# Naming the first layer's experts by a matrix product, and making the top-six mask by one comparison, in a two-layer diffusion transformer block

## The reference, cut to what matters

```python
def moe_ffn(h, router_w, router_bias, w_gu, w_down, shared_gu, shared_down):
    scores = jax.nn.sigmoid(jnp.dot(h, router_w, preferred_element_type=jnp.float32))
    _, idx = lax.top_k(scores + router_bias.astype(jnp.float32), TOP_K)       # TOP_K = 6 of 64
    gates = jnp.take_along_axis(scores, idx, axis=-1)
    gates = gates / jnp.sum(gates, axis=-1, keepdims=True) * ROUTED_SCALE
    ...
    def expert_block(args):
        src_b, gate_b, e = args
        y = swiglu(h_pad[src_b], w_gu[e], w_down[e])                          # 1024 -> 2*384 -> 1024
        return y * gate_b[:, None].astype(y.dtype)
    ...
    return routed + swiglu(h, shared_gu, shared_down)
```

## Time and profile before

| what | us |
|---|---|
| median of 3 runs (lowest, highest) | 2533.88 (2532.23, 2536.08) |
| the profiled execution | 2537.54 |
| its span in the trace | 2535.7 |
| TensorE matmul busy, whole span | 2305.1 |
| VectorE busy, whole span | 792.5 |
| mean DMA rate over the span | 301 GB/s |

### The profile page before, as it was taken

One profiled execution on the slowest core, in us unless ns is written; L12 is line 12 of the kernel. 1 busy time (PEld: TensorE's weight loads), 2 busy tenths in 40 slices (PEclk: granted clock), 3 DMA queues, 4 the chain that ended last, 5 costly groups with the idle time before them and its releaser, 6 DMA issues. The chain is left out here.

```text
span 2535.7 us, 40724 instructions
## 1 busy us (share of the span) xinstructions
PE 2305.1 (91%) x17170; PEld 1241.6 (49%) x17170; DVE 792.5 (31%) x1709; ACT 403.7 (16%) x860; POOL 229.0 (9%) x286
## 2 busy tenths in 40 slices
PE   6999899999877888888897998899999999999998
PEld 2456744454333343334343556755655565555553
DVE  2375745262110101111112546753222222212123
ACT  2323344110000000000001233352000000000000
POOL 0007200011101111110001005300000000000000
PEclk9999999999999999999998999999999999999999
DMA  8000197359999999999997310015999999999997
GB/s 333 34 17 36 65 379 305 135 226 413 427 426 417 417 419 417 417 419 399 385 422 303 129 50 21 28 47 212 404 390 377 376 423 367 429 412 424 408 416 297
DMA packets 86042, 762.18 MB, mean 301 GB/s; under 512 B 14376, under 2 KB 14904, under 8 KB 27232
## 3 DMA queue, kind: packets, MB, share of 16 engines
q1 hardware_dynamic: 74720, 734.30, 70.3%
q0 software_dynamic: 11136, 25.20, 2.6%
HBM read 748.54 MB, written 23.49 MB: 304 GB/s over the span
## 5 line engine op out<-in xcount | busy, mean ns | idle before, releaser
L1675 PE MATMUL banks<-arena,htreg 128*32 128x384 f32 (+2 forms) x5312 | 749.0, 521 | 119.0 <-DMA arena<-in_exp_w_gu 113.8
L1675 PEld LDWEIGHTS banks<-arena,htreg 128*32 128x32 f32 (+2 forms) x5312 | 331.7, 132 | 527.4 <-issue 435.1
L1700 PE MATMUL banks<-arena,modreg 128*32 128x512 f32 (+2 forms) x1992 | 351.6, 597 | 20.4 <-issue 19.1
L2556 DVE TENSOR_TENSOR modreg<-modreg,banks 128x384 f32<-128x384 f32 x65 | 36.0, 554 | 687.1 <-ACT modreg L2056 687.1
L1700 PEld LDWEIGHTS banks<-arena,modreg 128*32 128x32 f32 (+2 forms) x1992 | 117.4, 126 | 222.1 <-issue 220.7
L1715 PEld LDWEIGHTS banks<-htreg,hreg 128*128 128x128 f32 x800 | 194.2, 334 | 8.7 <-issue 5.9
L1715 PE MATMUL banks<-htreg,hreg 128*128 128x128 f32 x800 | 191.5, 398 | 0.0
L1196 PE MATMUL banks<-arena,htreg 128*128 128x512 f32 (+3 forms) x480 | 158.9, 490 | 0.0
L2079 ACT ACTIVATE modreg<-banks 128x512 f32<-128x512 f32 x58 | 34.7, 598 | 589.5 <-PE banks L1700 589.5
L2617 DVE COPY modreg<-banks 128x512 f32<-128x512 f32 x58 | 40.1, 692 | 268.5 <-PE banks L1700 268.5
L1196 PEld LDWEIGHTS banks<-arena,htreg 128*128 128x128 f32 x480 | 89.6, 191 | 65.0 <-issue 61.0
(11 more groups left out here) (439 smaller groups left out, 2235.3 us busy)
## 6 DMA issues: line engine op xcount, KB each, us to landing
arena<-in_exp_w_gu SPq DMA_DIRECT2D x256, 1536.0 KB, 17.3
arena<-in_exp_w_down SPq DMA_DIRECT2D x128, 1536.0 KB, 21.5
arena<-in_w_mod SPq DMA_DIRECT2D x32, 1024.0 KB, 9.9
modreg<-in_w_mod SPq DMA_DIRECT2D x14, 1024.0 KB, 8.0
arena<-y_d SPq DMA_DIRECT2D x4, 3072.0 KB, 17.8
modreg<-mod_d SPq DMA_DIRECT2D x20, 512.0 KB
arena<-in_shared_w_gu SPq DMA_DIRECT2D x6, 1536.0 KB
arena<-in_w_in SPq DMA_DIRECT2D x4, 2048.0 KB, 12.7
```

The source lines that it names most:

```text
L1675: last = mm(gu_bank(n, half)[rows, 0:DE], src[:, k, rows], up4[q][:, i, DE * half:DE * (half + 1)], start=(k == 0), stop=(k == KD - 1))
L1700: last = mm(ps[4 + half][rows, :], actT[:, k, rows], dn3[q][:, k, 512 * half:512 * half + 512], start=(k == 0), stop=(k == KE - 1))
```

## The change

**The mask** (both layers). After the biased scores VectorE takes only MAX8 for each tile, copies the six largest into `top6`, whose last two places hold a number that never occurs, strikes these six out of the scores with MATCH_REPLACE into `adr`, and compares: where a score and its struck-out copy differ, the mask is one. The positions and `onehot` are made after it (`experts_of_tokens`), in layer 0 right behind the mask, in layer 1 after the first expert unit's rows are copied.

**Counts ahead of the shared tile** (layer 0). `positions()` stands before `unit_part(1, "lo")`.

**Names by a product** (layer 0). One sorting round stays. From `rankcol` VectorE makes `by_rank` (64x64, one where an expert has a rank), and TensorE multiplies `index` with it behind `ranks()`, which gives the expert number of each rank in a row; VectorE copies ranks 8 to 63 into `eid` and tells SyncE. The seven later rounds are gone.

`index` moves from the table of layer 1 to the constants, which grow by one column. In the built program the arena thereby begins at byte 93,984 instead of 93,952.

```diff
-        cnt, key, rank, base, cap, left = (scratch(NE) for _ in range(6))
+        cnt, key, rank, base, cap = (scratch(NE) for _ in range(5))
+        top6 = scratch(NT, 8)
+        by_rank = carve(modreg, 2048 + DE + 1024, NE, part=NE)
...
+                def experts_by_rank():
+                    pe.wait_ge(order_made.sem, order_made.after(l, "perm"))
+                    mm(ps[1][0:1, 384:384 + NE], K("index")[0:NE], by_rank, start=True, stop=True).then_inc(order_psum.sem, 1)
+
...
                 else:
+                    positions()
                     unit_part(1, "lo")
-                    positions()
                     act_transposed(0)
                     ranks()
+                    experts_by_rank()
                     unit_down(0)
                     unit_part(1, "hi")
                     lists_by_expert()
...
                     dve.wait_ge(order_made.sem, order_made.after(LAST, "rank"))
+                    experts_of_tokens()
                     gates_made()
...
                 link(dve.memset(mask[:, n_t, :], 0.0))
+                link(dve.memset(top6[:, nt_, TOPK:], 3e38))
                 dve.wait_ge(order_act.sem, order_act.after(l, "scores"))
                 link(tt(selb[:, nt_, :], scores[:, nt_, :], bc(srow("rbias"), 1, n_t), ALU.add))
                 for i in range(n_t):
                     link(dve.max(out=top8[:, i, :], in_=selb[:, i, :]))
-                    link(dve.max_index(out=idx8[:, i, :], in_max=top8[:, i, :], in_values=selb[:, i, :]))
-                link(dve.tensor_copy(idxf[:, nt_, :], idx8[:, nt_, :]))
+                link(dve.tensor_copy(top6[:, nt_, 0:TOPK], top8[:, nt_, 0:TOPK]))
                 for i in range(n_t):
-                    link(tt(onehot[:, i], bc(K("experts"), 1, TOPK), bc(idxf[:, i, 0:TOPK], 2, NE), ALU.is_equal))
-                    ins = red(mask[:, i, :], onehot[:, i].rearrange("p k e -> p e k"), AX, ALU.add)
-                    if i < n_t - 1:
-                        link(ins)
-                    else:
-                        ins.then_inc(order_made.sem, 1)
+                    link(dve.match_replace(out=adr[:, i, :], in_to_replace=top6[:, i, :], in_values=selb[:, i, :], imm_value=-3e38))
+                tt(mask[:, nt_, :], selb[:, nt_, :], adr[:, nt_, :], ALU.not_equal).then_inc(order_made.sem, 1)
+
+                def experts_of_tokens():
+                    for i in range(n_t):
+                        link(dve.max_index(out=idx8[:, i, :], in_max=top8[:, i, :], in_values=selb[:, i, :]))
+                    link(dve.tensor_copy(idxf[:, nt_, :], idx8[:, nt_, :]))
+                    for i in range(n_t):
+                        link(tt(onehot[:, i], bc(K("experts"), 1, TOPK), bc(idxf[:, i, 0:TOPK], 2, NE), ALU.is_equal))
+
+                if l < LAST:
+                    experts_of_tokens()
                 unit_times(0)
...
-                left_of = [key]
-
-                def sorted_round(j):
-                    link(dve.max(out=next8, in_=left_of[0]))
-                    ins = dve.max_index(out=eid[:, 8 * j:8 * j + 8], in_max=next8, in_values=left_of[0])
...
-                sorted_round(0)
+                link(dve.max(out=next8, in_=key))
+                dve.max_index(out=eid[:, 0:8], in_max=next8, in_values=key).then_inc(sorted_ready.sem, 1)
                 link(ts(row64[lo64], key[lo64], keycol[lo64], None, ALU.is_gt))
                 link(red(rankcol[lo64], row64[lo64], AX, ALU.add))
+                ts(by_rank, K("experts")[lo64], rankcol[lo64], None, ALU.is_equal).then_inc(order_made.sem, 1)
...
                 link(dve.tensor_copy(rank, ps[0][:, 0:NE]))
+                dve.wait_ge(order_psum.sem, order_psum.after(l, "eid"))
+                dve.tensor_copy(eid[0:1, 8:NE], ps[1][0:1, 392:384 + NE]).then_inc(sorted_ready.sem, 1)
...
-                for j in range(1, NE // 8):
-                    sorted_round(j)
```

More of the change, by code:

```diff
@@ L70 @@
                ("sin_hd", 2 * 6 * HD), ("cos_pe", 2 * HEADS * MLA_ROPE), ("sin_pe", 2 * HEADS * MLA_ROPE),
-               ("experts", NE), ("slot_no", P), ("codes", NT * CODES)):
+               ("experts", NE), ("slot_no", P), ("codes", NT * CODES), ("index", 1)):
     CONST[_n] = (_at, _at + _w)
@@ L96 @@
 _at = 0
-for _n, _w in (("col_rank", N_COL), ("col_from", N_COL), ("marked", P), ("slot_of", 4), ("index", 1)):
+for _n, _w in (("col_rank", N_COL), ("col_from", N_COL), ("marked", P), ("slot_of", 4)):
     TABLE[_n] = (_at, _at + _w)
@@ L146, in constants @@
     put("slot_no", np.arange(P)[None, :])
+    put("index", np.arange(P)[:, None])
     token = np.arange(P)[:, None, None] + P * np.arange(NT)[None, :, None]
@@ L158, in constants @@
     row("slot_of", ROUTED_MARK + np.stack([p, p - 96 * (p >= 96), p % 64, p % 32], axis=1))
-    row("index", p[:, None])
     return a
@@ L632, in after @@
                 return self.counter.at(l, self.names[l].index(step) + 1)
-        order_psum = Order("order_psum", ("router", "pos", "rank", "list"),
+        order_psum = Order("order_psum", ("router", "pos", "rank", "eid", "list"),
                            ("router", "pos", "marks", "eid", "places", "shares", "rank"))
-        order_made = Order("order_made", ("mask", "beats", "listT"), ("mask", "perm", "beats", "shares", "rank"))
+        order_made = Order("order_made", ("mask", "beats", "perm", "listT"), ("mask", "perm", "beats", "shares", "rank"))
         order_act = Order("order_act", ("scores",), ("scores", "marks", "shares"))
@@ L1557, in marks @@
                     last.then_inc(order_psum.sem, 1)
+                def experts_by_rank():
+                    pe.wait_ge(order_made.sem, order_made.after(l, "perm"))
+                    mm(ps[1][0:1, 384:384 + NE], K("index")[0:NE], by_rank, start=True, stop=True).then_inc(order_psum.sem, 1)
                 def order_of_experts():
                     pe.wait_ge(order_made.sem, order_made.after(LAST, "perm"))
-                    mm(ps[0][0:1, P:P + N_COL], T_("index")[0:NE], perm, start=True, stop=True).then_inc(order_psum.sem, 1)
+                    mm(ps[0][0:1, P:P + N_COL], K("index")[0:NE], perm, start=True, stop=True).then_inc(order_psum.sem, 1)
                     pe.wait_ge(order_act.sem, order_act.after(LAST, "marks"))
@@ L2760, in _ @@
                 ts(beats[lo64], key[lo64], keycol[lo64], None, ALU.is_lt).then_inc(order_made.sem, 1)
-                left_of = [key]
-                def sorted_round(j):
-                    link(dve.max(out=next8, in_=left_of[0]))
-                    ins = dve.max_index(out=eid[:, 8 * j:8 * j + 8], in_max=next8, in_values=left_of[0])
-                    if j in (0, NE // 8 - 1):
-                        ins.then_inc(sorted_ready.sem, 1)
-                        dve.wait_ge(sorted_ready.sem, sorted_ready.at(l, 1 if j == 0 else 2))
-                    else:
-                        link(ins)
-                    if j < NE // 8 - 1:
-                        link(dve.match_replace(out=left, in_to_replace=next8, in_values=left_of[0], imm_value=-1e9))
-                        left_of[0] = left
-                sorted_round(0)
+                link(dve.max(out=next8, in_=key))
+                dve.max_index(out=eid[:, 0:8], in_max=next8, in_values=key).then_inc(sorted_ready.sem, 1)
                 link(ts(row64[lo64], key[lo64], keycol[lo64], None, ALU.is_gt))
                 link(red(rankcol[lo64], row64[lo64], AX, ALU.add))
+                ts(by_rank, K("experts")[lo64], rankcol[lo64], None, ALU.is_equal).then_inc(order_made.sem, 1)
                 link(ts(dropcol[lo64], rankcol[lo64], float(U_), -float(U_ - W_ - G_), ALU.is_ge, ALU.mult))
```

## The result

The kernel before took 2536.1 us, the changed one 2547.9 us (medians of seven runs each); the ratio is 1.0043, 95% interval 1.0032 to 1.0055, so 10.9 us slower by the ratio (8.1 to 13.9), which is the figure used from here on; the medians themselves lie 11.8 us apart. Forecast were 2537.9 us, +4.0 us, and a range that ended at 2541.0. The profiled run of the changed kernel has a span of 2545.7 us, 10.0 us more than the one of before. The two traces can be laid side by side, instruction by instruction.

The account below looks back on a forecast made before the run. TensorE was taken to set the pace until about 598 us, then DMA in layer 0's expert stage. 0 + 2.3 (gather) + 1.7 (clock) = +4.0 us, from 2533.9 to 2537.9 us; range 2530.8 to 2541.0.

Parts of the forecast that it names:

- What bounds the kernel: Layer 0: TensorE sets the weight stream until about 598 us, after it the stream sets TensorE; weight waits from about 649.
- Mask, counts, product, SyncE: Layer 0 routing: mask 5.3 us earlier, first load at 531.5 us, shared down product 1.05 us ahead; covered, 0 in the sum.
- The gather: Layer 0, unit 2: first gather beside early loads lands 10 us after issue, transposes at 562.2 instead of 559.87: +2.3 us.
- The clock: Layer 0, behind TensorE's wait for the gather: one half-clock spell nearly certain, +1.7 us, 3.0 if the longer one.
- rival (d): Unit 2's transposes and first half: wait long enough for the 6.7 us half-clock spell, 2.3 + 3.0 = 5.3, 2539.2 us; chance 0.13.
- The layout: Weight ring in layer 0 moved from byte 93,952 to 93,984: no term in the sum, only a rival at +2.0 us.
- rival (e): Layer 0 weight loads: one more column of constants moves the ring, +2.0 us on top, near 2540; chance 0.06.
- Layer 1: Mask some 2 us earlier, but counts stand behind the shared unit; moved comparisons fall into VectorE idle time: zero.
- The sum again: Whole kernel: 0 (mask, counts, rank product) + 2.3 (gather) + 1.7 (clock) = +4.0 us.

## Why the prediction was wrong, point by point

**What bounds the kernel.** Right. TensorE sets the pace before 598 us, and DMA in the stage behind: the lag at 592.60 us goes through the stage unshortened, the loads that came earlier only moved the hole to 570 to 600 us, and TensorE first waits for weights at 650.8 us (651.80 less the 1.0 us of late start; forecast about 649).

**Mask, counts, product, SyncE.** Right. Less the 1.0 us by which the run starts late, the first load goes out at 530.7 (forecast 531.5), the shared down product at 532.4 (532.5), the sixth and seventh load at 535.1 and 535.6 (536.4), and on TensorE the product delays nothing beside the others. That it needs the earlier counts as cover the forecast did not say: without them TensorE waits 0.70 us for it. Whether it then costs more than the lead it lacks the times don't show (+6.3 us, 3.0 to 9.6, with 5.5 expected).

**The gather.** Right: it lands 9.9 us after issue (forecast 10), and less the 1.0 us of late start the transposes begin at 562.0, +2.2 against +2.3. The Trainium skill, DMA: Bandwidth & Descriptors, Queues, rings and completion order, has the engines take turns by packets. The trace fits that: 128 rows are eight for each of 16 engines, and one weight packet of 460 ns ahead of each is 3.7 us, an estimate, on top of the 2.2 us that the same packets took without loads; they took 5.3 us beside weights. The 4.3 us to its first packet, against 1.7 beside no loads, are not given by it.

**The clock.** The mechanism was right, the term was mis-sized: +1.7 us in the sum, 3.3 in the profiled run (5.45 less 2.2) and 2.4 in the change without its column. It was sized by the spell of 3.3 us around 554 us, where the idle time ahead was 0.67 us. The forecast wait of 3.4 us was already too long for that price: waits of 2.96 to 3.17 us lost 2.5 to 2.8 us here. The 3.0 of rival (d), taken from the spell behind an idle 3.79 us, was the nearer row.

**The layout.** This is the step that failed. The sum had 0, rival (e) +2.0 with a chance of 0.06; measured are +4.6 to +4.8 us in three kernels that differ from the one before in nothing else. The forecast gave it little because windows of like load differ by 1.7%, where a quarter per cent would not stand out, and because no row had large loads at such a start. Both are so, and neither is a reason to put the term at nothing: a stage at the pace of DMA adds up every tenth of a per cent of rate, and rows that can't show an effect can't exclude it. By the estimate from the Trainium skill (same page, How a descriptor splits into AXI transactions) 32 bytes would be one beat in 384, 0.26% or 2.0 us, and 64 and 128 bytes two and four times as much. The page tells this of bytes that are fetched, while the ring is where the loads write. The traces agree in the sign and that the boundary is 256 bytes; they show 0.4 to 0.5% of rate with 32 bytes and less, not more, with 64 and 128.

**Layer 1.** Right: from the last gather of layer 0 to the end the lag changes by 0.9 us, downwards, less than the executions of one kernel differ by (2541.6 to 2548.3 us for the changed one).

**The sum again.** 2.2 (gather) + 2.4 to 3.3 (clock) + 4.6 to 4.8 (layout) = 9.2 to 10.3 us, with 10.9 measured (8.1 to 13.9) and 10.0 between the profiled runs. The parts found one by one lie inside the interval; the 1.0 us ahead of 520 us is not traced to a cause, and runs with the old layout began as late (the change without its column by 1.3 us).

## What to carry to other kernels

When an edit adds a constant, look where the buffers behind it come to lie. Here the target of the large loads was best on a multiple of 256 bytes, and one column of constants cost about as much as the rest of the edit. Before an idle stretch of the DMA engines is filled, ask which small transfer lives in it: loads that nobody needs soon were better held here until it had landed, and TensorE's wait for it cost a half clock besides. Time the parts of a change apart: here two of them were a gain and were buried under the others. And before a half clock is put down to an idle stretch, look whether other executions with the same stretch have it.

## What the runs showed of the hardware

- Large loads (rows of 12,288 bytes) into SBUF that starts 32 bytes past a multiple of 256 had packets of 462 to 464 ns (median) instead of 460, and 0.4 to 0.5% less rate with all 16 engines busy; the kernel took 4.6 to 4.8 us longer, and 4.8 us longer with 64 bytes.
- Instruction packets of 16 KB beside them grew far more, from 935 to 950 ns to 1020 to 1068, in all five kernels off the boundary and in none of the nine on it. Why they do is open; 141 of them, 0.12 us longer each, would be about 1 us spread over 16 engines, an estimate.
- A gather of 128 rows, the first of the stage, took 4.3 to 4.8 us from issue to landing beside no loads and 9.6 to 9.9 us beside weight loads, 2.5 us of the difference ahead of its first packet (4.2 us after issue instead of 1.7).
- An idle stretch of 0.67 us between two short pieces of work was followed by the half clock in nine of twelve traces and not in the other three; idle waits of 2.96 to 4.86 us were followed by it in all five.
